# A decoder step on one core: queries scored against centred keys, the first two expert choices reordered, the sample rows' dot products spread out

## What is computed

```python
q = (xb @ w_q).reshape(blk, PEER_HEADS, 2, half)
mu = jnp.mean(q, axis=-1, keepdims=True)
q = (q - mu) * lax.rsqrt(jnp.mean(jnp.square(q - mu), axis=-1, keepdims=True) + LN_EPS)
s = jnp.einsum('thpd,hpnd->thpn', q, keys_f)
s1, i1 = lax.top_k(s[:, :, 0], PEER_TOPK)
s2, i2 = lax.top_k(s[:, :, 1], PEER_TOPK)
...
idx = e1 * PEER_NKEYS + e2
gate = jax.nn.softmax(sc, axis=-1)
h = jax.nn.gelu(jnp.einsum('thkd,td->thk', u_tab[idx], xb))
return jnp.einsum('thk,thkd->td', gate * h, v_tab[idx])
```

## Time and profile before

| | us |
|---|---|
| median of 3 runs | 1863.81 |
| the profiled execution | 1866.73 |
| its span in the profile | 1864.9 |
| TensorE matmul busy | 1427.4 (77%) |
| VectorE busy | 1176.2 (63%) |
| ScalarE busy | 427.6 (23%) |
| GpSimd busy | 1002.7 (54%) |
| gathers' queue q0: bytes, share of the 16 DMA engines' span | 546.94 MB, 74.5% |
| weights' queue q1: bytes, share | 123.88 MB, 17.2% |

### The profile page before, as it was taken

The page is one execution under the profiler, slowest core; times in us unless marked ns, Lnnn a source line. Parts: engine busy times, 40 slices in busy tenths (PEclk is TensorE's granted clock), DMA queues, the critical chain, the costliest instruction groups (busy, mean ns, idle before and its releaser), DMA issues.

```text
span 1864.9 us, 21193 instructions
## 1 busy us (share of the span) xinstructions
PE 1427.4 (77%) x7320; PEld 900.8 (48%) x7320; DVE 1176.2 (63%) x3036; ACT 427.6 (23%) x861; POOL 1002.7 (54%) x1067
## 2 busy tenths in 40 slices
PE   8999998999889799889994896355644335675477
PEld 7888897876555365557662563022411001241033
DVE  1120227967778755775768665878888868776642
ACT  2320202224442121332211222111222211121022
POOL 0000002655565555555566666676777776767765
PEclk9999999999997799889996998657765666587599
DMA  7335635999999999999999999999999999999997
GB/s 295 136 122 217 225 114 203 354 413 411 401 400 414 413 383 412 411 412 380 408 404 383 388 410 413 409 408 407 408 409 409 404 407 391 396 364 409 408 378 291
DMA packets 173191, 672.23 MB, mean 360 GB/s; under 512 B 20727, under 2 KB 24439, under 8 KB 159262
## 3 DMA queue, kind: packets, MB, share of 16 engines
q0 software_dynamic: 151520, 546.94, 74.5%
q1 hardware_dynamic: 21494, 123.88, 17.2%
q10 hardware_dynamic: 72, 0.07, 0.0%
HBM read 663.40 MB, written 7.41 MB: 360 GB/s over the span
## 4 chain that ended last, share of the span: by engine, by line
PE 45%; DMA 22%; DVE 16%; POOL 9%; issue 6%; ACT 2%; SPq 0%; DVEq 0%; POOLq 0%; PEldq 0%
PE PJ L1739 16%; DMA at<-in_v_tab,idxV 14%; PE PJ L1612 9%; DMA at<-in_u_tab,idx 8%; PE Y L1789 7%; DVE at L1470 7%; POOL at L767 5%; POOL at L758 4%; PE PJ L1596 4%; PE PJ L1623 2%; DVE at L1340 1%; PE PJ L1698 1%; PE PJ L1683 1%; PE PJ L1705 1%; PE PJ L1689 1%
## 5 line engine op out<-in xcount | busy, mean ns | idle before, releaser
L758 POOL DMA_INDIRECT at<-in_u_tab,idx x512 | 488.3, 954 | 533.8 <-DVEq L1358 297.7
L1470 DVE CUSTOM_DVE_ANT_0 at<-at,XD 128x1024 f32<-128x1024 f32 x512 | 614.5, 1215 | 187.0 <-DMA at<-in_u_tab,idx 177.0
L767 POOL DMA_INDIRECT at<-in_v_tab,idxV x512 | 488.4, 954 | 306.4 <-PE Y L1789 172.2
L1789 PE MATMUL Y<-at,at 128*32 128x512 f32 x1920 | 334.5, 824 | 347.0 <-DMA at<-in_v_tab,idxV 346.9
L1739 PE MATMUL PJ<-at,at 128*128 128x264 f32 (+2 forms) x1920 | 417.8, 377 | 6.7 <-ACT at L837 3.1
L1739 PEld LDWEIGHTS PJ<-at,at 128*128 128x128 f32 x1920 | 348.8, 194 | 82.3 <-issue 20.5
L1789 PEld LDWEIGHTS Y<-at,at 128*32 128x32 f32 x1920 | 68.5, 133 | 528.6 <-issue 526.1
L1612 PE MATMUL PJ<-at,at 128*128 128x256 f32 (+2 forms) x960 | 222.4, 390 | 7.7 <-issue 4.4
L1612 PEld LDWEIGHTS PJ<-at,at 128*128 128x128 f32 (+2 forms) x960 | 168.0, 178 | 62.4 <-issue 16.5
L1596 PE MATMUL PJ<-at,at 128*128 128x256 f32 (+1 forms) x640 | 143.1, 382 | 0.0
L1596 PEld LDWEIGHTS PJ<-at,at 128*128 128x128 f32 (+1 forms) x640 | 107.6, 170 | 36.4 <-issue 10.0
(11 more groups left out here) (278 smaller groups left out, 1373.2 us busy)
## 6 DMA issues: line engine op xcount, KB each, us to landing
at<-in_w_blk SPq DMA_DIRECT2D x72, 1024.0 KB, 8.0
at<-in_w_q SPq DMA_DIRECT2D x16, 1024.0 KB, 8.1
at<-in_w_o SPq DMA_DIRECT2D x8, 1024.0 KB, 7.7
at<-in_u_tab,idx POOLq DMA_INDIRECT x512, 11.4
at<-in_v_tab,idxV POOLq DMA_INDIRECT x512, 11.0
at<-in_state SPq DMA_DIRECT2D x4, 1024.0 KB, 8.3
out_st_s<-at SPq DMA_DIRECT2D x4, 1024.0 KB, 8.2
at<-in_w_pg SPq DMA_DIRECT2D x2, 2048.0 KB, 13.4
```

What stands on the lines that cost most here:

```text
L758: pool.indirect_dma_start(ubuf[slot], None, u_tab, bass.IndirectOffsetOnAxis(rows_of, 0)).then_inc(u_in[slot], 16)
L767: pool.indirect_dma_start(vbuf[slot], None, v_tab, bass.IndirectOffsetOnAxis(rows_of, 0)).then_inc(v_in[slot], 16)
L1470: v.tensor_tensor_reduce(out=t, in0=t, in1=XD[:, :], scale=1.0, scalar=0.0, op0=ALU.mult, op1=ALU.add, accum_out=hraw[:, n % 2, k:k + 1]). ...
L1789: last = mm(Y[32 * c:32 * c + 32, s, :], wpadV[d // PAIR % 2][:, g, :], vbuf[slot][:, 512 * s:512 * s + 512], start=False, stop=final)
```

## The change

Seven edits go together:

- **Centred keys.** The keys, not the queries, lose their mean: each of four products (`keys`, 128 by 512) multiplies four key blocks by `center` = identity - 1/128 (made by VectorE once), and ScalarE copies the result over the keys. The queries are turned as they are. Only the reciprocal of the deviation remains; ScalarE applies it when it copies the scores, in two instructions of 128 columns in the place of one of 256. `q turn` now waits for the query block alone, and the copy of the scores waits for the reciprocal (`rsr_ok`). The two normalising instructions and the product on VectorE are gone.
- **Where the key products stand.** The first is ahead of the first choice, behind the output blocks of tile 0; the other three stand at slot (-1, 7), behind the output blocks of tile 1.
- **Second statistics later.** The turn of the first choice comes ahead of its statistics, its scores ahead of the second query block, and the second choice's statistics behind part 4 of the first choice.
- **Parts 2 and 3 of the second choice** move behind the first dot products, to slots 1 and 2 (all five parts in slots 1 to 5). `late rows` move to slot 1, the taken blocks to slots 2, 3, 5 and 6, tile 1's norm to slots 12 and 14 (before 8 and 10).
- **The copy of tile 0's rows** to PSUM (L1466) moves from ahead of the first dot product to right behind the norm of tile 0.
- **The first v gathers** start two slots earlier (`FIRST_V`), behind output block 1 of tile 1 in the place of block 3.
- **Samples.** The sample dot products stand in every fourth slot of iterations 25 and 26, in the place of every second slot of 26, and the rest of tile 2 starts at slot (27, 6), not (27, 1).

```diff
-FIRST_V = {divmod(k - 3, TOPK): k for k in range(VB)} | ...
+FIRST_V = {divmod(k - 5, TOPK): k for k in range(VB)} | ...
-SAMPLE_DOTS_AT, SAMPLE_SUMS_AT = 26, 28
-REST_AT = {0: 18, 1: 20, 2: 27, NT: 30}
+SAMPLE_DOTS_AT, SAMPLE_SUMS_AT, SAMPLE_STEP = 25, 28, 4
+REST_AT = {0: (18, 1), 1: (20, 1), 2: (27, 6), NT: (30, 1)}
...
-            put(choice(0, 1)[6:], -1, (1, 3, 5))
+            put(choice(0, 1)[4:], -1, (1, 2, 3, 4, 5))
...
-    out = mixers(0) + wo[0][:2] + [("first stats",)] + wo[0][2:] + x1[0] + bra1[:1] + turn(0, "t1", 0) + wq[:1]
-    out += first[:2] + wq[1:2] + first[2:4] + second[:2] + bra1[1:2] + first[4:5] + second[2:3] + bra1[2:6] + first[5:]
-    out += second[3:4] + bra1[6:] + second[4:6] + wq[2:3] + wo[1]
+    out = mixers(0) + wo[0][:2] + [("first stats",)] + wo[0][2:] + x1[0] + [("row copy", 0)] + keys[:1] + bra1[:1] + turn(0, "t1", 0) + wq[:1]
+    out += first[2:3] + first[:2] + first[3:4] + wq[1:2] + first[4:5] + bra1[1:2] + second[2:3] + bra1[2:5] + first[5:7]
+    out += second[:2] + bra1[5:6] + first[7:] + second[3:4] + bra1[6:] + wq[2:3] + wo[1]
...
-    behind = spread_over(wq[3:PH] + ...
+    behind = spread_over(keys[1:] + wq[3:PH] + ...
...
-    for k, events in zip((0, 1, 3, 4, 6, 8, 10), taken):
+    for k, events in zip((1, 2, 3, 5, 6, 12, 14), taken):
...
-                        pool.wait_ge(pj_done, JOB["job", 0, "wo", 3, 1] + 1)
+                        pool.wait_ge(pj_done, JOB["job", 0, "wo", 1, 1] + 1)
...
-                elif part == 1:
-                    act.wait_ge(nmr_ok, r + 1)
-                    for i in range(2):
-                        half = q[:, 128 * i:128 * i + 128]
-                        act.activation(half, half, ACT.Identity, scale=rsR[:, i:i + 1],
-                                       bias=mvR[:, i, 0:1]).then_inc(qn_ok, 1)
...
-                act.activation(scores, R[:, 256:512].rearrange("p (a b) -> p a b", a=2), ACT.Copy).then_inc(sc_ok, 1)
+                act.wait_ge(rsr_ok, r + 1)
+                for i in range(2):
+                    last = act.activation(scores[:, i, :], R[:, 256 + 128 * i:384 + 128 * i], ACT.Copy, scale=rsR[:, i:i + 1])
+                last.then_inc(sc_ok, 1)
...
+            v.tensor_scalar(center, ident[:, :], -1.0 / 128, None, ALU.add).then_inc(center_ok, 1)
...
-                    link(v.reciprocal(rsR[0:p, :], sdR[0:p, :]))
-                    mean = mvR[:, :, 0:1].rearrange("p a b -> p (a b)")
-                    v.scalar_tensor_tensor(out=mean, in0=mean, scalar=-1.0, in1=rsR[:, :], op0=ALU.mult,
-                                           op1=ALU.mult).then_inc(nmr_ok, 1)
+                    if r:
+                        v.wait_ge(sc_ok, r)
+                    v.reciprocal(rsR[0:p, :], sdR[0:p, :]).then_inc(rsr_ok, 1)
...
+                elif name == "keys":
+                    pe.wait_ge(keys_in, 16)
+                    pe.wait_ge(center_ok, 1)
+                    last = mm(out, center, keysT[:, 4 * i:4 * i + 4, :], start=True, stop=True)
...
-                pe.wait_ge(qn_ok, 2 * r + 2)
+                pe.wait_ge(pj_act, ACT_DONE["job", group(j), "wq", h if j < NT else 4 * h + 3, j])
...
-                pe.wait_ge(keys_in, 16)
+                pe.wait_ge(pj_act, ACT_DONE["job", 0, "keys", h // 2 if j < NT else 2 * h + 1])
```

More of the change, by code:

```diff
@@ L42 @@
 FIRST_SUMS = {(1, 3): 0, (1, 6): 4, (1, 10): 8, (1, 15): 12}
-FIRST_V = {divmod(k - 3, TOPK): k for k in range(VB)} | {(1, k + 1): k for k in range(VB, 12)} | {(1, k + 2): k for k in (12, 13)} | {
+FIRST_V = {divmod(k - 5, TOPK): k for k in range(VB)} | {(1, k + 1): k for k in range(VB, 12)} | {(1, k + 2): k for k in (12, 13)} | {
     (2, k - 14): k for k in (14, 15)}
@@ L49, with sample_at @@
 SAMPLE_ROUTES_AT = 19
-SAMPLE_DOTS_AT, SAMPLE_SUMS_AT = 26, 28
-REST_AT = {0: 18, 1: 20, 2: 27, NT: 30}
+SAMPLE_DOTS_AT, SAMPLE_SUMS_AT, SAMPLE_STEP = 25, 28, 4
+REST_AT = {0: (18, 1), 1: (20, 1), 2: (27, 6), NT: (30, 1)}
+def sample_at(n, k):
+    b, odd = divmod(TOPK * (n - SAMPLE_DOTS_AT) + k, SAMPLE_STEP)
+    return b if odd == 0 and b in range(S) else None
 def group(j):
@@ L261, in plan @@
     wq2 = queries(1)
-    behind = spread_over(wq[3:PH] + turn(0, "t1", 1) + wq[PH:] + mixers(1) + close + wq2[:1], (-1, 7), (13, 6))
+    behind = spread_over(keys[1:] + wq[3:PH] + turn(0, "t1", 1) + wq[PH:] + mixers(1) + close + wq2[:1], (-1, 7), (13, 6))
     behind.update(spread_over(wq2[1:], (13, 10), (15, 15)))
@@ L274, in plan @@
     for j, at in REST_AT.items():
-        behind.setdefault((at, 1), []).append(("order", j))
+        behind.setdefault(at, []).append(("order", j))
         for k, e in enumerate(rest(j)):
-            behind.setdefault((at, k + 2), []).append(e)
+            behind.setdefault(divmod(TOPK * at[0] + at[1] + 1 + k, TOPK), []).append(e)
             if e[2] == "pe":
-                behind.setdefault((at, k + 4), []).append(("take", e))
+                behind.setdefault(divmod(TOPK * at[0] + at[1] + 3 + k, TOPK), []).append(("take", e))
     taken = [[("late rows",)]] + [[("take", e)] for e in wo[1]] + [[e] for e in x1[1]]
-    for k, events in zip((0, 1, 3, 4, 6, 8, 10), taken):
+    for k, events in zip((1, 2, 3, 5, 6, 12, 14), taken):
         behind[-1, k] = events + behind.get((-1, k), [])
@@ L285, in plan @@
         for k in range(TOPK if n <= ITERS else LAG):
-            if n == SAMPLE_DOTS_AT and k % 2 == 0:
-                out.append(("sample dot", k // 2))
+            if sample_at(n, k) is not None:
+                out.append(("sample dot", sample_at(n, k)))
             if n == SAMPLE_SUMS_AT and k == 0:
@@ L316, in plan @@
                 out += [("masks",), ("compact",)]
-            b = (TOPK * (n - SAMPLE_DOTS_AT) + k + 1) // 2
-            if k % 2 and b in range(S):
-                out += [("job", 1, "row", b, s) for s in range(2)]
+            if sample_at(n, k + 1) is not None:
+                out += [("job", 1, "row", sample_at(n, k + 1), s) for s in range(2)]
             out += choices.get((n, k), [])
@@ L376, in u_number @@
 def u_number(n, k):
-    before = k // 2 + 1 if n == SAMPLE_DOTS_AT + 1 else S if n > SAMPLE_DOTS_AT else 0
-    return n * TOPK + k + before
+    behind = (n - SAMPLE_DOTS_AT - 1) * TOPK + k
+    return n * TOPK + k + (min(behind // SAMPLE_STEP + 1, S) if behind >= 0 else 0)
 def u_sample(b):
-    return U_SAMPLE + 3 * b
+    return U_SAMPLE + (SAMPLE_STEP + 1) * b
 def v_number(n, k):
@@ L589, in decoder_step @@
         scaled_ok = sem("scaled_ok")
+        center_ok = sem("center_ok")
         clear_ok, first_ok = sem("clear_ok"), sem("first_ok")
@@ L784, in _ @@
                         pool.wait_ge(first_ok, k // (TOPK // 2) + 1)
-                    if n == SAMPLE_DOTS_AT and k % 2 == 0:
-                        gather_u(u_sample(k // 2), idxT[:, FIRST + k // 2:FIRST + k // 2 + 1])
+                    b = sample_at(n, k)
+                    if b is not None:
+                        gather_u(u_sample(b), idxT[:, FIRST + b:FIRST + b + 1])
                     if n + 1 < ITERS:
@@ L873, in evacuate @@
                     head_outputs(NT, i, 1, S, src)
+                elif name == "keys":
+                    act.activation(keysT[:, 4 * i:4 * i + 4, :], src.rearrange("p (a b) -> p a b", a=4), ACT.Copy).then_inc(
+                        pj_act, 1)
                 elif name in ("normv", "norm1", "norm2"):
@@ L927, in route @@
             def route(j, h, part):
-                r, q = ROUTE[j, h], q_of(j, h)
+                r = ROUTE[j, h]
                 if part == 0:
@@ L1515, in _ @@
                     count(v.bn_stats(bn[0][:, 0, :], x1[:, 0, 0:512]))
+                elif what == "row copy":
+                    row_copy(*args)
                 elif what == "late rows":
```

19 lines of the change are left out of this document (11 added, 8 removed).

## The result

The changed kernel takes 1868.33 us (median of 12 runs, 1863.5 to 1875.2); the kernel before, run beside it, 1865.07 us (12 runs). The ratio is 1.0026, with a 95% interval of 1.0013 to 1.0038. On another chip the pair gave 1868.42 against 1863.94 us, ratio 1.0025 (1.0014 to 1.0036). So the change costs 3.3 and 4.5 us by the medians, 4.8 and 4.7 by the ratios, where I forecast a gain of 4. The difference is inside my half a percent, and the time inside my range, but the sign is wrong and two sets of runs agree on it. The profiled executions hardly show it (1866.73 before, 1868.96 and 1865.82 after; I call the last two the first and the second profile of the changed kernel): on these chips one execution of a kernel lies up to 7 us from its median.

The account below looks back on a forecast made before the run. The prediction took the gathers' data flow at some 410 GB/s as the bound, so only its start and dips count. Ramp -2.8 and samples -1.2 us sum to -4.0, from 1863.8 to 1859.8 us, range 1849 to 1869.

Parts of the forecast that it names:

- First choice: Turning tile 0's queries without waiting for statistics brings the first gather to 297.3 us, 2.7 us earlier; scores' copy pair 0.7 us.
- First key product and row copy: Ahead of the first choice and in 285 to 290 us: both hidden, costed at nothing; the product 0.9 us if uncovered.
- First dot product: VectorE's first dot product in the ramp starts at 307.6 us in the place of 312.28, 4.7 us earlier.
- Tile 1's output blocks: TensorE starts them at about 314.4 us after 1.8 us idle, four in 14.0 us with the clock at 1.00.
- the clock falls in the ramp all the same: Rival, chance 0.10: TensorE is 1.1 us behind in the ramp, which then gives 0; time 1862.6 us.
- Ramp: Start-up until about 340 us: VectorE's lead taken as the gain, -2.8 us, with bounds of -1.1 and 3.8.
- Three key products at 2.8 us of TensorE: Behind tile 1's four output blocks: 3 x 0.94 us, cutting TensorE's lead from 4.3 to 1.5 us.
- Samples: Iterations 25 and 26: spreading the sample dot products gains a third of 3.6 us, -1.2 us; bounds -3.6 and +3.6.
- The slower rival: Chance 0.13: sample rows wait behind every sum and the dip comes in iterations 25 and 26; +4.9 us, 1868.7.
- Lead given back: Rival, chance 0.20: the ramp's lead at 341 us is lost later, leaving -1.2 us alone, 1862.6.
- Middle dips close: Rival, chance 0.20: half of some 12 us lost in slices 14, 18, 21 and 22 is regained; -10 us, 1853.8.
- Sum: Whole kernel: -2.8 for the ramp and -1.2 for the samples, -4.0 us, giving 1859.8 us.

Follow-up runs that it names:

- the turn first: Changed kernel with choice (0,3)'s statistics and root one slot later, behind tile 1's turn: 1860.86 us, ratio 0.9988 to before on the chip at 1864 us.
- the old samples: Changed kernel with choice (0,3)'s statistics one slot later and sample work back in its places of before: 1860.87 us, ratio 0.9982 to before.
- centring alone, with the turn first: Kernel before with only centred keys added and choice (0,3)'s statistics one slot later: 1864.69 us, ratio 1.0005 to before.

## Why the prediction was right or wrong

- **First choice**: predicted first gather 297.3 us. The profile of the first pair has 299.39, that of the second run of the same kernel 297.5. The difference is TensorE's clock at the first query block: in the first profile it is granted 0.66 from 285 to 290 us and 16 multiplies take 4.94 us, in the second 1.00 and 3.62 us. The two rows of that window, first the first profile, then the second:

```profile
285.00:290.00 5.00, 4.18 (x16) 3.40 (x16) 2.38 (x3) 1.19 (x2) 0.00 (x0) 0.66 0.00 0
```
```profile
285.00:290.00 5.00, 4.18 (x23) 3.37 (x21) 2.13 (x3) 1.19 (x2) 0.00 (x0) 1.00 0.00 0
```

  The instructions and the idle gaps ahead are the same (1.13 and 0.82 us), and 0.25 of the 1.9 us between the two first gathers were there at 281 us already. So the step was right, and this clock is a matter of the execution. The pair of scores' copies took 0.62 us, nearer 0.38 to 0.88's middle than my 0.7; with the reciprocal ready it started 0.41 us behind the scores. The Trainium skill ("ScalarE: Activation LUTs", What ACT_TABLE_LOAD costs) gave an estimate of 680 ns for the pair, as I had worked it out; the row is 9% below that.
- **First key product and row copy**, costed at nothing: right. The product took 1.02 us at 280.95.
- **First dot product**: predicted 307.6; 307.40 in the second profile, 309.33 in the first.
- **Tile 1's output blocks**: predicted from 314.4, idle 1.8 us ahead, four blocks in 14.0 us at full clock. Measured 314.19 in the second profile, 316.12 in the first, with the same length and the same gap in both:

```profile
316.12 14.05 PE L1626 MATMUL PJ<-at,at 128*128 128x256 f32 x64 [1.84 <-issue]
```

  with the clock at 1.00 from 315 to 320 us, where before had 0.50. The rival that the clock falls in the ramp all the same is out. It fell later, in the stall (0.51 from 360 to 365 us).
- **Ramp, -2.8 us**: near as far as 340 us, and not kept. The ledger has the changed kernel 3.3 us ahead there in the second profile (1.7 in the first), between my bounds of -1.1 and 3.8. But the sign that I named, a rate above 300 from 320 to 340 us, did not come: it is 277 and 275 (before 223), and the dip stands between 325 and 335 us with 217 and 152 GB/s. The term that I put at nothing is "tile 1's norm pushed behind four more dot products". GpSimd waits 4.0 us for it, TensorE's turn of tile 1 twice (0.58 and 0.82 us), and TensorE's forecast lead of 1.5 us is gone: with the turn first it starts tile 1's query blocks at 352.29, before at 351.88. The turn-first kernel keeps 0.8 to 1.5 us in the ledger until 640 us, and 3.1 us below before in the medians of that chip (interval of the ratio: 4.7 us below to 0.2 above).
- **Three key products at 2.8 us of TensorE**: the step that failed, together with the sentence that the rest costs "nothing from 340 us to the end by itself". I priced them by TensorE's time and by the instructions they add. That price was 0.9 us short: they take 3.7 us, from 330.01 to 333.73, since two of them wait 0.3 us for a free PSUM bank. It isn't what cost the time, for the turn-first kernel pays it too. What I left out is that they stand at the head of a list dealt out by summed cost, so all behind them changes its place against steps with fixed slots. I listed new waits and who is queued behind them, but only for waits that the diff adds. The wait that hurt is an old one: `[7.26 <-DVE mvR L1413]` stood in the trace of before, harmless because t1 was not behind it. Put behind it, t1 cost TensorE 6.7 us and the gelu behind it VectorE 13.0, together 7.6 us of time. The text's own sign of error, "a new dip in 340 to 400 us", is what came.
- **Samples, -1.2 us**: not resolved by the runs. The windows of 1580 and 1640 us are no longer dips in the second profile (337 to 408, 325 to 406), but 1540 to 1580 and 1660 to 1700 lose instead: 383, 398 and 355, 367 for before's 409, 409 and 390, 409. Summed from 1540 to 1680 us, the loss against 410 GB/s is 9.0 us before and 4.5 and 5.0 in the changed kernel; with the turn first it is 5.1, and 6.2 with the old samples added. The last pair is near my 1.2, in one trace of each, while the medians are 1860.86 and 1860.87. The slower rival's standstills came: VectorE waits 16.7 us in 9 waits for the broadcast rows (longest 4.5), where before had 13.7 in 6. What it expected of them did not: GpSimd's longest wait for a dot product there is 1.6 us (before 3.2), and no window of 20 us falls below 355 GB/s. Its 1868.7 is near the measured 1868.33 by luck, as the loss came at 340 to 420 us.
- **Lead given back**: not this case, as the turn-first kernel shows. **Middle dips close**: ScalarE's busy time fell from 427 to 406.6 us, and part of the dips of 840 and 1020 us did go, 5 to 6 us in the ledger. But centring alone, with the turn first, is at 1.0005, so nothing of this reaches the time there. Whether it does with the rest of the change I can't separate.
- **Sum**: with the failed step mended the change gives 1860.9 where before is 1863.9, -3.1 for -4.0. That nearness is in part luck: the interval reaches from -4.7 to 0.2, the ramp's lead had shrunk to some 1 us by 400 us, and most of what that execution leads by 1040 us (8.4 in the ledger) comes from 640 to 1040 us, where the forecast had nothing. Nor is that trace typical: it is 3.7 us below its kernel's median.

## What to carry to other kernels

When an edit adds work to a list that a planner deals out by cost, print the plan of both kernels and compare the order on every engine, not the cost of what was added. In the trace of before, look for long waits of an engine that isn't the bound, and ask who may not come to stand behind them: a copy that frees TensorE belongs ahead of a step that waits 7 us for VectorE. A second stall further down (here the gelu behind block copies) can double the price of the first. When a step moves later, ask also which buffers come free with it: here a norm four slots later holds GpSimd for 4 us. With a difference of 0.3%, one profiled execution tells the place but not the size.

## What the runs showed of the hardware

- The granted clock of one and the same program differed between executions: 0.66 or 1.00 in the window from 285 to 290 us, with the same instructions ahead. It moved the first gather by some 1.7 us (299.39 against 297.46, less the 0.25 us that stood before).
- Chips differ by 8 to 10% on the same kernel: before takes 1863 to 1865 us in three groups, and 2019.5 and 2042.6 us in the others. The rate rows of the turn-first kernel, first on a chip at 2019 us, then on one at 1864 us:

```profile
GB/s 285 119 145 231 189 64 310 318 412 392 340 390 399 400 404 382 413 411 384 384 406 310 411 408 408 396 354 328 345 351 358 369 356 340 366 358 386 352 311 162
```
```profile
GB/s 297 137 117 218 232 114 226 325 413 411 403 403 412 414 412 412 410 412 411 411 403 375 393 410 413 409 408 409 407 409 409 405 409 389 398 401 398 408 369 279
```

  The peak is the same, some 412, but in slices 26 to 36 the first stays at 328 to 386. The bytes are the same. No run here shows the cause. The Trainium skill ("Perfetto Trace Analysis", Roofline) states 358 GB/s as a core's share of memory when both cores of a pair use it, and more for a core alone; the stretch lies about that figure, but what ran beside the kernel no trace here shows. It matters for the reading: on such chips the changed kernel was at 0.9940 to 0.9977 of before, on the others at 1.0025. The verdict on a change of a few us can turn with the chip, while, by the medians, the difference between the changed kernel and its mended form kept its sign on all three chips where both ran side by side (6.8, 12.3 and 7.6 us).
